# One block for the convolution's output projection and the FFN: seven half-size products for 20 of 22 gate/up pairs

## What is computed

```python
def short_conv_mixer(h, w_in, w_conv, w_out):
    ...
    return (gate_b * conv) @ w_out

def swiglu(h, w_gate_up, w_down):
    g, u = jnp.split(h @ w_gate_up, 2, axis=-1)
    return (jax.nn.silu(g) * u) @ w_down

def second_block(...):
    ...
        x = x + g_m[:, None, :] * rms_norm_2(h, norm_gains[i, 1])
        h = modulate(rms_norm_2(x, norm_gains[i, 2]), sh_f, sc_f)
        h = swiglu(h, ffn_w_gate_up[i], ffn_w_down[i])
        x = x + g_f[:, None, :] * rms_norm_2(h, norm_gains[i, 3])
```

## Time and profile before

| | us |
|---|---|
| median of three runs | 2809.53 (2806.56 to 2810.03) |
| profiled execution, its own time | 2805.2 |
| its span, first to last instruction | 2803.0 |
| from the first matmul of the projection (1884.0) to the end | 919.0 |
| PE busy over the span | 2449.5 (87%) |
| DVE busy | 1633.9 (58%) |
| ACT busy | 1195.1 (43%) |
| POOL busy | 295.5 (11%) |
| mean granted clock of TensorE | 0.932 |

### The profile page before, as it was taken

The page is one execution under the profiler, slowest core; times in us unless marked ns, Lnnn a source line. Parts: engine busy times, 40 slices in busy tenths (PEclk is TensorE's granted clock), DMA queues, the critical chain, the costliest instruction groups (busy, mean ns, idle before and its releaser), DMA issues. The chain is left out here.

```text
span 2803.0 us, 32318 instructions
## 1 busy us (share of the span) xinstructions
PE 2449.5 (87%) x11004; PEld 1963.4 (70%) x11004; DVE 1633.9 (58%) x1863; ACT 1195.1 (43%) x1465; POOL 295.5 (11%) x248
## 2 busy tenths in 40 slices
PE   2889986898895799999997599989599999599998
PEld 2657764677574687777775478867488878488876
DVE  5368884655775799999996654442433322433323
ACT  2236664565421677777774611111333322333312
POOL 0000001887110100000001100000000000000000
PEclk9899996999896899999998699999799999799999
DMA  5131221339462999999998533322133332233322
GB/s 198 46 109 39 53 76 55 101 92 355 128 224 90 371 399 398 398 398 399 397 397 298 207 109 109 98 79 94 45 97 92 102 88 78 90 91 103 90 90 90
DMA packets 295707, 474.61 MB, mean 169 GB/s; under 512 B 18706, under 2 KB 169679, under 8 KB 295119
## 3 DMA queue, kind: packets, MB, share of 16 engines
q1 hardware_dynamic: 269104, 376.95, 38.9%
q0 software_dynamic: 20192, 75.55, 8.2%
q10 hardware_dynamic: 6336, 21.11, 1.9%
HBM read 407.49 MB, written 60.82 MB: 167 GB/s over the span
## 5 line engine op out<-in xcount | busy, mean ns | idle before, releaser
L255 PE MATMUL f_ps<-f_h,f_w 128*128 128x512 f32 x2112 | 483.9, 392 | 4.7 <-DVE f_h L2792 4.7
L2151 DVE TENSOR_TENSOR e_w<-e_raw,e_w 128x1024 fp32r<-128x1024 f32 x384 | 441.6, 1217 | 58.9 <-ACT e_w L2215 58.8
L255 PEld LDWEIGHTS f_ps<-f_h,f_w 128*128 128x128 f32 x2112 | 399.7, 189 | 88.9 <-issue 5.5
L2215 ACT ACTIVATE e_w<-e_raw 128x1024 fp32r<-128x1024 f32 x384 | 375.9, 1050 | 190.2 <-PE e_pgu L255 155.6
L2775 DVE TENSOR_TENSOR f_w<-f_raw,f_w 128x1024 fp32r<-128x1024 f32 x132 | 161.7, 1225 | 436.8 <-ACT f_w L2732 436.8
L255 PE MATMUL e_pgu<-e_w,e_xt 128*128 128x512 f32 x1536 | 368.3, 396 | 15.5 <-DVE e_xt L2159 9.1
L255 PEld LDWEIGHTS e_pgu<-e_w,e_xt 128*128 128x128 f32 x1536 | 285.2, 189 | 90.4 <-DVE e_w L2151 18.0
L2732 ACT ACTIVATE f_w<-f_raw 128x1024 fp32r<-128x1024 f32 x132 | 139.6, 1058 | 318.3 <-PE f_ps L255 296.6
L255 PE MATMUL s_ps<-h,s_w 128*128 128x512 f32 x1152 | 267.3, 394 | 5.5 <-DVE h L2551 5.5
L255 PEld LDWEIGHTS s_ps<-h,s_w 128*128 128x128 f32 x1152 | 219.0, 190 | 52.3 <-DVE h L2551 5.9
L255 PE MATMUL f_ps<-f_w,f_a 128*128 128x512 f32 x1056 | 244.2, 394 | 7.3 <-DVE f_a L2804 7.3
(11 more groups left out here) (350 smaller groups left out, 3249.8 us busy)
## 6 DMA issues: line engine op xcount, KB each, us to landing
e_raw<-in_w_expert_gate_dram SPq DMA_DIRECT2D x128, 512.0 KB, 7.9
e_raw<-in_w_expert_up_dram SPq DMA_DIRECT2D x128, 512.0 KB, 7.3
e_raw<-in_w_expert_down_dram SPq DMA_DIRECT2D x128, 512.0 KB, 7.2
f_raw<-in_ffn_w_gate_up_dram SPq DMA_DIRECT2D x88, 512.0 KB, 3.8
f_raw<-in_ffn_w_down_dram SPq DMA_DIRECT2D x44, 512.0 KB, 3.5
y_rows<-am_zrow SPq DMA_DIRECT2D x4, 4352.0 KB, 34.2
raw_rows<-in_w_ada_dram POOLq DMA_DIRECT2D x32, 512.0 KB, 4.0
y_rows<-e_yo ACTq DMA_DIRECT2D x32, 512.0 KB, 6.3
```

The costliest lines, as they stand in the source:

```text
L255: o = pe.matmul(out, stat[i], mov[j], start=start and n == 0, stop=stop and n == 2)
L2151: dve.tensor_tensor(w[1][:, slot % CUT], raw[:, slot], w[0][:, slot % CUT].bitcast(F32), ALU.subtract).then_inc(low, 1)
L2215: act.activation(w[0][:, slot % CUT], raw[:, slot], ACT.Copy).then_inc(high, 1)
```

## The change

`project_rows` and `feed_forward` are replaced by one block, `conv_out_ffn`, with tiles w_*.

- **Projection.** The first three tiles go over the eight chunks of K together, the other five one after the other. The weights arrive through four buffers instead of two, behind the broadcast of the norm gain. After each tile (from tile 3 on) PE does `turn`: eight 128x128 transposes of one normalised tile of rows (w_unit). The norm of the new residual is thus taken per tile, on ACT (`square`, `x_square`, `scale`, `affine`) and DVE (`evict`, `inverse`), beside the projection of the next tiles. The residual rows go back to memory (SP) instead of staying in the core, and come back as one 4 MB load before the last stage.
- **Gate and up** run over all 1024 tokens at once. Take for one chunk of 128 FFN channels the 2x2 matrix whose rows are gate and up and whose columns are the halves of K, and for h the 2x2 matrix of K halves and token halves. Twenty chunks are computed by seven products of a 128x512 by a 512x512 block (`strassen`, 7 x 4 x 3 = 84 matmuls) instead of eight (96). The left sides are weights or sums of them (`first_sums`, `third_sum`, `fourth_sum`: four DVE operations of 128x512 for a chunk), the right sides are B11, B21, T2, T1, T3, B22, T4, made once (t1 to t4, then `right_leading` and `right_rest`, 128x2048 each). The results are recombined by DVE from PSUM (`c11`, `second_u`, `fourth_u`, `c22`, `c12`, `gated`: nine operations of 128x512), with one copy by ACT (`keep_p1`). Two chunks are computed as before (`classic`): their first token half before the twenty, the second behind.
- **Left operands** go through a ring of seven slots of 128x512 (w_ring, `leading` on ACT and `rest` on DVE), one for each product.
- **Activations** of each chunk are written to memory (g.a_dram, POOL queue) and read back for `w_down` in pieces of 256 KB, four buffers deep; each piece is then split by ACT and DVE beside the w_down row block. The down products keep their count, 2 x 22 x 24 matmuls.
- **Places.** B11, B21, the split down weights (d_w) and the split activations (a_t) lie in the memory of y_1 (from 155616, 32 past a multiple of 64), T4 in that of y_0. w_ring (109696, 124032), T1, T2, T3 and B22 (in w_out, from 27776 and 60544) lie at multiples of 64.

The core of the diff:

```diff
-def project_rows(nc, g, tag, src, w_dram, gate, x_from, x_keep, gain):
...
-def feed_forward(nc, g, a, out):
...
+def conv_out_ffn(nc, g, a, y_t, y_at, out):
...
+    NC = 2
+    NS = KF - NC
+    N0 = 4 * NC
+    N1 = N0 + 7 * NS
...
+        ring = [ctx.enter_context(nc.sbuf_tensor(f"w_ring{j}", [P, 7, KH, P], F32R)) for j in range(2)]
...
+        B11, B21 = pair_of(y_t[1], lo_half), pair_of(y_t[1], hi_half)
+        T2, T1 = pair_of(wo[0], lo_half), pair_of(wo[0], hi_half)
+        T3, B22 = pair_of(wo[1], lo_half), pair_of(wo[1], hi_half)
+        T4 = (y_t[0][:, back, hi_half], y_t[0][:, back, lo_half])
+        t2, t1, t3, t4 = of[0][:, back, lo_half], of[0][:, back, hi_half], of[1][:, back, lo_half], b21
+        right = (B11, B21, T2, T1, T3, B22, T4)
+        s_tmp = [h[:, k, lo_half].rearrange("p (k n) -> p k n", k=KH) for k in range(4)]
...
+        a_t = [[y_t[1][:, 4 + c, lo_half] for c in range(4)], [y_t[1][:, 4 + c, hi_half] for c in range(4)]]
...
+                def store(s, f, b, cols):
+                    pool.wait_ge(acted, s + 1)
+                    pool.dma_start(g.a_dram[ds(f, 1)].squeeze(0)[:, cols], act_rows[:, b, cols]).then_inc(a_out[b], 16)
...
+                def turn(n):
+                    pe.wait_ge(unit_done, n + 1)
+                    if n:
+                        pe.wait_ge(h_done, n)
...
+                        o = pe.transpose(ps[:, 6 + k // 4, (k % 4) * P:(k % 4 + 1) * P], unit[:, k * P:(k + 1) * P], g.ident[:])
+                    o.then_inc(turned, 1)
+                def product(n, bank, left, moving, start, stop):
+                    pe.wait_ge(low, n + 1)
+                    for k in range(KH):
+                        o = three_passes(pe, ps[:, bank, :], [v[:, left, k, :] for v in ring], [v[:, k, :] for v in moving],
+                                         start and k == 0, stop and k == KH - 1)
+                    o.then_inc(used, 1)
...
+                def strassen(i, b):
+                    n = N0 + 7 * i
+                    first = isinstance(i, int) and i == 0
+                    if not first:
+                        pe.wait_ge(c22_done, i)
+                    for q in range(7):
+                        pe.wait_ge(b_low, q + 1)
+                        if first and q in (4, 6):
+                            pe.wait_ge(acted, q // 2 - 1)
+                        elif not first and q == 4 + 2 * b:
+                            pe.wait_ge(c12_done, i)
+                        elif not first and b == 0 and q == 5:
+                            pe.wait_ge(c21_done, i)
+                        product(n + q, bank(b, q), q, right[q], True, True)
...
+                for n in range(3, NT):
+                    pe.wait_ge(scaled if n == 3 else xsq, n - 2)
+                    for c in range(2):
+                        for k in range(KD):
+                            o = out_part(n, k, c)
+                        if c == 0 and n in (4, 5):
+                            turn(2 * n - 7)
+                    o.then_inc(done, 1)
+                    turn({3: 0, 4: 2, 5: 4, 6: 5, 7: 6}[n])
+                pe.wait_ge(xsq, 6)
+                classic(0, (4, 5), B11, B21, 1, 2)
+                turn(7)
+                pe.wait_ge(h_done, NT)
+                classic(4, (6, 7), B11, B21, 1, 2)
+                pe.wait_ge(xsq, NT)
+                strassen(0, 0)
+                pe.wait_ge(acted, NC)
+                with pe.Fori(0, NS // 2 - 1) as j:
+                    strassen(2 * j + 1, 1)
+                    strassen(2 * j + 2, 0)
+                strassen(NS - 1, 1)
+                pe.wait_ge(c21_done, NS - 1)
+                pe.wait_ge(p1_out, NS)
+                classic(N1, (6, 7), T1, B22, 8, 8)
+                pe.wait_ge(u2_done, NS)
+                classic(N1 + 4, (0, 1), T1, B22, 8, 8)
+                for hh in range(2):
                     for f in range(KF):
-                        pe.wait_ge(low, PIECES * h + 2 * KF + f + 3)
-                        for n in range(NH):
+                        t = KF * hh + f
+                        pe.wait_ge(d_low, t + 1)
...
+                def c22(i, b):
+                    dve.wait_ge(x_done, i + 1)
+                    dve.wait_ge(used, N0 + 7 * i + 5)
+                    dve.tensor_tensor(u2, u2, ps[:, bank(b, 4), :], ALU.add).then_inc(u3_done, 1)
+                    dve.tensor_tensor(c22_at, x, ps[:, bank(b, 4), :], ALU.add).then_inc(c22_done, 1)
...
+                def gated(i, b, r):
+                    dve.wait_ge(used, N0 + 7 * i + 7)
+                    dve.wait_ge(u3_done, i + 1)
+                    dve.tensor_tensor(u2, u2, ps[:, bank(b, 6), :], ALU.add).then_inc(c21_done, 1)
+                    dve.wait_ge(a_out[b], 16 * r)
+                    dve.wait_ge(s11, i + 1)
+                    dve.wait_ge(c21_done, i + 1)
+                    dve.tensor_tensor(act_rows[:, b, lo_half], sg[0], u2, ALU.mult)
+                    dve.wait_ge(s12, i + 1)
+                    dve.wait_ge(c22_done, i + 1)
+                    dve.tensor_tensor(act_rows[:, b, hi_half], sg[1], c22_at, ALU.mult).then_inc(acted, 1)
...
+                def pair(i, b, r, r_next):
+                    gated(i - 1, 1 - b, r)
+                    next_rest(i, b, 6)
+                    first_sums(i + 1, 1 - b, r_next)
+                    c11(i, b)
+                    next_rest(i + 1, 1 - b, 0)
+                    next_rest(i + 1, 1 - b, 1)
+                    third_sum(1 - b)
+                    fourth_sum(i + 1, 1 - b)
+                    second_u(i, b)
+                    next_rest(i + 1, 1 - b, 2)
+                    fourth_u(i, b)
+                    next_rest(i + 1, 1 - b, 3)
+                    c22(i, b)
+                    next_rest(i + 1, 1 - b, 4)
+                    c12(i, b)
+                    next_rest(i + 1, 1 - b, 5)
...
-                project_rows(nc, g, "pc_", lambda k: [x[:, k, :] for x in y_t], a["conv_w_out_2"][0], g.gate2[:, 0, :],
-                             g.x_dram, g.x, a["norm_gains_2"][0, 1])
-        clear_sems(nc, g)
-        with x4:
-            feed_forward(nc, g, a, out)
+                conv_out_ffn(nc, g, a, y_t, y_at, out)
```

781 lines of the change are left out of this document (560 added, 221 removed).

## The result

| | before | after |
|---|---|---|
| median, us | 2808.05 (2805.33 to 2810.03, 4 runs) | 2685.34 (2683.93 to 2686.73, 4 runs) |
| span of the profiled execution | 2803.0 | 2682.2 |
| first projection matmul to the end | 919.0 | 795.6 |
| mean granted clock | 0.932 | 0.945 |

The ratio is 0.9566, with a 95% interval of 0.9553 to 0.958. The kernel is 123 us faster; 102 were forecast. The kernel before was run once more, which moves its median from 2809.53 to 2808.05. The rewritten part, from the first projection matmul on, is 123.4 us shorter, and it starts 2.6 us later.

A forecast was written before the change was run, and what follows sets the result against it. TensorE was taken to bound the stages, with gaps between them hanging on VectorE. Matmuls 774.6, turns 8.0, waits 14.4, clock 6.7, tail 12.0 and start 1.5 gave 817.2 against 919.0, so 2708 us; range 2684 to 2740.

The forecast's parts named there:

- Matmuls of down: Down stage: 1056 matmuls at 0.241 us, both operands at 32 past 64 and the costs adding up; 254.6 us.
- not at all in gate/up and down: Rival: operand places cost nothing in these stages, 20.8 us less, 2687; chance 0.25 shared with costing once in down.
- The other matmuls: Projection 90.0 us, twenty chunks of 19.3 us making 385.8, two classic chunks 22.4 and 21.8.
- Turns: Transposes between projection tiles: eight groups of eight, each delaying the next matmul about 1.0 us; 8.0 us.
- Waits: TensorE idle at tile 3, turns 1 and 3, after tile 7's turn, making right sides, middle of down; 14.4 us.
- The right sides: Making them before the first Strassen chunk's product 6: VectorE needs 35.5 us, TensorE 27.7; waits of 8.6 in all.
- Clock and small latencies: Lower granted clock behind waits: 1.7 us at the start, 5 at tile 7's turn and the right sides; 6.7.
- tail: End of the kernel: as before, but 1.3 us less because the root's table is already loaded; 12.0 us.
- start: Start of the projection: the 512 KB gain broadcast stands ahead of the first weight on SP; +1.5 us.
- hand over later than I walked: Rival: VectorE and ScalarE slower at right sides and in the tile chain; 2720 to 2740, chance 0.2.
- VectorE becomes the bound: Rival: in the steady loop slower VectorE operations set the period, kernel ends slower, 2875 at twice 0.69; chance 0.03.
- The change doesn't do what it says: Rival: for instance products run one by one in the twenty chunks because a bank is held; 2750, chance 0.02.

The follow-up runs named there:

- the edit of the last transposes: The changed kernel with tile 7's transposes in banks 0 and 1 instead of 6 and 7, so the second classic chunk starts right behind them; 2685.66 us.

## Why the prediction was right, and which step failed

Laid beside each other over the stretch from 1884.0 to the end, 817.2 was forecast and 798.2 came (2682.2 - 1884.0). The terms:

- **Matmuls of down, -15.2.** This is the step that failed: "I take 0.241". With 0.2268, 1056 of them are 239.4. The prediction read from four slow and fast stretches that a place 32 past 64 costs, and added it up for two operands. The rows told only of pairs in which the operands stood differently, and of pairs in which both stood at a multiple of 64. The third kind, both alike but elsewhere, was not in them. Cost by difference fitted as well as cost by place did, and was not among the rivals. What the runs showed in its place: the cost hangs on the difference of the two starts modulo 256, which is 0 in down, and down went to 0.2333 as soon as one operand was moved. The time came out near that of the rival "not at all in gate/up and down", 2687, by luck, since the other errors made up for the rest, and that rival had it wrong too: in the loop the place costs what was forecast (period 19.3 forecast, 19.33 measured). A total near a rival's doesn't make the rival true.
- **The other matmuls** came as forecast: a chunk costs 0.04 more, 0.8 in twenty. So did their number, and 56.0 measured for an eighth product confirms the price of a chunk.
- **Turns, about -1.** A turn costs 0.79 to 0.84 behind its start, the 0.8 of the earlier trace rows, and 0.9 with what is lost ahead of it; of the 0.2 added for the change of kind half was there.
- **Waits, -4.4.** The walk had 0.5, 0.5, 3.3, 8.6 and 1.5. Measured: 0.24 at tile 3, nothing at turns 1 and 3, 2.99, 5.34, 1.42. The right sides are the one large miss. VectorE's chain was sized well: from the end of ScalarE's affine (2000.4) to the start of product 6 (2037.16) it is 36.8, forecast 35.5. But TensorE would not have been at product 6 after 27.7 even without waits, since the clock fell on the way: 18.35 us for the 72 matmuls behind the wait, where 17.05 are normal, and 4.56 for 12, where 2.98 are. Without these 2.9 us the three waits would have been 8.2, an estimate, and 7.9 was forecast for them. The prediction charged the wait and the clock one on top of the other. The clock's loss shortens the wait behind it, as the edit of the last transposes shows from the other side.
- **Clock and small latencies** some +0.5 (what is left over, not measured), **tail** 11.2 instead of 12.0, **start** 2.6 instead of 1.5 behind 1884.0. The load of the gain was given 1.5.
- **Outside the span** lie 3.4 of the 22.7 (the rest of it, 0.3, is rounding): the median stands 3.1 above the profiled span, not 6.5 as with the run before.

Of the rivals, "hand over later than I walked" is refuted by the loop's rows and the turns, and by the chain of the right sides, 36.8 where 35.5 was forecast and not 30% more. "VectorE becomes the bound" had the right bound: no operation of the loop's rests took longer than 0.694, seven more for a chunk changed nothing, and fourteen more made VectorE the bound. The Trainium skill (SBUF — State Buffer, section SBUF: two separate sides) lets VectorE, in some of its operations, and GpSimd exclude each other; beside one store for each chunk from GpSimd's queue the trace shows none of it. "The change doesn't do what it says" is refuted by 84 matmuls in each period.

The rule of the Trainium skill (TensorE: Matmul & The Clock Gate, Part 2) that weights and moving data come through independent ports leaves no cost for the place of an operand, which made down the 239.4 of a rival; the trace agrees there, with 0.2268. It does not agree with 0.2338 in the loop. The runs bear it out as long as both operands agree modulo 256.

## What to carry to other kernels

When stretches of equal matmuls run at different spacings, tabulate the start addresses of both operands, and test each reading on a pair that no stretch shows yet, here by moving one tensor by 32 bytes. For matmuls of this form, align stationary and moving operands to the same remainder of 256; 352 bytes of padding gave 11.6 us in a kernel that runs three-pass matmuls nearly all the time. And where two engines meet at a chain, take the later of the two arrival times: a wait or a slow clock ahead of that point is not to be added to the wait at it.

## What the runs showed of the hardware that was not expected

- 128x512 fp32r matmuls with their weight loads stand 0.2267 us apart when both operands' starts agree modulo 256 bytes (up to 0.2275 beside others that don't), and 0.2289 to 0.2343 when they don't, at a full granted clock. Moving either operand alone can make it slower or faster.
- VectorE's 128x512 additions are 0.68 to 0.69 long in the trace and start every 0.60 in a dense stream, 0.72 when the second waits for the first. Lengths of rows overstate a dense stream by 13%.
- The clock behind a wait of one length varies. Behind 3.64 us the first 4.6 us had a granted clock of 0.63 and 13 matmuls in one half and 0.50 and 11 in the other half of one execution; behind 2.99 us 0.69 and 14 in one kernel, 1.00 and 20 in another.
- Waits near 1 us inside a busy stretch cost little beside themselves: behind the 1.03 us at 2550.34 the next 48 matmuls take 11.19, where 47 x 0.2268 + 0.39 = 11.05, and behind the 1.02 at 2037.16 the next 36 take 8.90, where a row of the loop takes 8.58. The granted clock is 1.00 in both.
